# Key-query scores shared by both directions of an mLSTM recurrence, and the causal mask as one rounded matrix pass

## The chip, the cores and the metric

The kernel runs on one core of a Trainium2 chip. A core has TensorE (matrix products into the accumulator memory PSUM), VectorE, ScalarE, GpSimd, SyncE and DMA queues; each engine works through its own instructions in order, and semaphores make one wait for another. The metric is the device time of one launch in microseconds (us), lower is better. Before the change it was 3623.95 us, the median of 3 runs (3618.31 to 3626.76).

## The reference

Two networks run one after the other. The first has two layers; in each, the 512 tokens and 256 context tokens are projected, and three mixers work on the result: a Fourier mix, an mLSTM recurrence in both directions, and an attention. An output projection and an MLP follow. The second network (two layers of another kind) is not touched. The recurrence is what the change is about:

```python
def step(carry, inp):
    C, n, m = carry
    qb, kb, vb, ib, fb = inp
    b = jnp.cumsum(fb, axis=-1)
    dmat = jnp.where(tri, b[..., :, None] - b[..., None, :] + ib[..., None, :], -jnp.inf)
    inter = b + m[..., None]
    m_t = jnp.maximum(inter, dmat.max(axis=-1))
    w_intra = jnp.exp(dmat - m_t[..., None])
    w_inter = jnp.exp(inter - m_t)
    s = jnp.einsum("bhtd,bhsd->bhts", qb, kb) * w_intra
    num = jnp.einsum("bhts,bhsv->bhtv", s, vb) + w_inter[..., None] * jnp.einsum("bhtd,bhdv->bhtv", qb, C)
    den = s.sum(axis=-1) + w_inter * jnp.einsum("bhtd,bhd->bht", qb, n)
    h = num / jnp.maximum(jnp.abs(den), jnp.exp(-m_t))[..., None]
    ...
    C_new = decay[..., None, None] * C + jnp.einsum("bhs,bhsd,bhsv->bhdv", wk, kb, vb)
```

`fwd` and `bwd` take the same `q`, `k` and `v`; only the gates, the mask (`tri`, lower or upper) and the order of the chunks differ. There are 4 heads of 96 features.

## The kernel before

All work is float32. Most large products are done as three rounded passes (`hi` and `lo` parts of a number, in a type that TensorE takes in one pass, fp32r); the small ones of the recurrence are true float32 products, and the trace shows each such matmul as two TensorE records.

`build` calls, for each of the two layers, `fourier`, `latent_attention`, `mlstm_inputs`, `mlstm` (here), `out_projection` and the MLP. Each is a block of instructions with a part for every engine; no block begins before the one before it is through on all engines, so nothing of `out_projection` runs beside `mlstm`. No weights are loaded inside `mlstm`; the only DMA is a small table (`select`).

`mlstm` works on tiles of 128 tokens. There are `TT` = 6 of them (`LT` = 4 latent tiles, 0 to 3, and 2 of context, 4 and 5). `ORDER` walks them as 4, 5, 0, 1, 2, 3 forward and 5, 4, 3, 2, 1, 0 backward. `steps_all` is the list of twelve steps, forward and backward in turn: u = 2 i + d is position i of direction d. `outs` are the steps that give an output: all 12 in the first layer, and in the second, where the context is no longer needed, the 8 from i = 2 on. `upds` are the 10 steps that update a state (i below 5). An output step does:

- `weigh(u)` on TensorE, three groups of matmuls: the mask (L1715, one matmul of the 128 x 128 identity with the mask spread over 4 heads, 128 x 512), the selection of the row exponents (L1718, 4 matmuls with 36 rows), and the key-query scores (L1724, 4 matmuls with 96 rows). Mask and selection add up in one PSUM bank, the scores have another; both pairs of banks alternate;
- ScalarE takes the exponential of the first bank (L1786, 4 instructions);
- VectorE multiplies scores and weights (L1817, `scored_step`);
- `sums(u)` on TensorE: products with the values (L1736, 128 rows), and, for i above 0, with the state (L1742, 96 rows);
- VectorE combines and normalises (`combine`, L1828 to L1844) and signals `written`; TensorE's next `sums` waits for that;
- `grow(u)` on TensorE (L1753, 128 rows), with keys weighted by GpSimd (L1691), and VectorE's `pass_on` (L1856, L1858) update the state;
- where a tile has been visited from both sides, VectorE adds up its squares (`moments`, L1865, L1866).

The order is written out by hand. TensorE runs, for each step, `weigh` of the next output step, then `sums` and `grow` of this one. VectorE runs `scored_step` of the next output step, then `combine`, `pass_on` and, where due, `moments` of this one. After the last step the normed tiles are gated, turned on TensorE (L1771) and copied (L1796).

Below, an output step is a first visit if its tile has not been seen by the other direction, and a second visit otherwise. In the first layer the twelve are F F S S F F F F S S S S, in the second F F F F S S S S.

Of the kernel before, what the change touches and what calls it, by code (L numbers as in the profile page):

```python
# [20 lines left out]
F32R = mybir.dt.float32r  # L21
ALU = mybir.AluOpType
ACT = mybir.ActivationFunctionType
AX = mybir.AxisListType

P = 128
D = 1024
KT = D // P
# [3 lines left out]
ALL = LAT + CTX  # L32
LT, CT = LAT // P, CTX // P
TT = LT + CT

F_GROUP = D // 16
M_HEADS, M_DIM = 4, 3 * D // 32
# [44 lines left out]
C_IDENT, C_LOWER, C_UPPER, C_DFT, C_END = 0, P, 2 * P, 3 * P, 5 * P  # L82
# [1540 lines left out]
    k_turned.close(TT)  # L1623


def mlstm(core, arena, scratch, m, mix, ctx_out):

# [8 lines left out]
    a = Alloc(scratch, 4192 + ROWS * TT)  # L1638
    weight, score = a(2, M_HEADS * P), a(2, M_HEADS * P)
    keyed = a(2, hid)  # L1640
    part, both = a(1, M_HEADS * (M_DIM + 1)), a(2, M_HEADS * (M_DIM + 1))
    state = a(2, M_HEADS * (M_DIM + 1))
    den, ms = a(2, M_HEADS), a(1, TT * M_HEADS)[:, 0, :]
    sq = a(1, hid)[:, 0, :]
    ai = m.rows_i[0:ROWS, :]
    tile = lambda ap, t: ap[:, t * P:(t + 1) * P]
    scale = float(M_DIM) ** -0.5
# [4 lines left out]
    upds = [u for u, (d, i, t) in enumerate(steps_all) if i < TT - 1]  # L1652

    done_at = lambda t: max(u for u in outs if steps_all[u][2] == t)
    tiles_done = sorted(range(nt), key=done_at)
    n_out = lambda u: sum(v < u for v in outs)
    n_upd = lambda u: sum(v < u for v in upds)
# [4 lines left out]
    turned = core.counter("gate_rows_turned")  # L1662
    select_in = core.counter("select_in")
    weights_p = core.counter("weight_exponents")
    scores_p = core.counter("mlstm_scores")
    w_exp = core.counter("weights_ready")
    scored = core.counter("weighted_scores")
    summed = core.counter("mlstm_sums")
# [7 lines left out]
    with nc.Block(no_gpsimd_drain=True) as block:  # L1676
# [19 lines left out]
        @block.tensor  # L1696
        def _(pe):
            for q, rows in enumerate((ai, m.w_state, m.floor, m.w_key)):
                for t in range(TT):
                    n = q * TT + t  # L1700
                    last = nc.tensor.transpose(core.ps[:, 4 + n // 12, n % 12 * ROWS:(n % 12 + 1) * ROWS],
                                               tile(rows, t), core.ident(ROWS))
            last = nc.tensor.matmul(core.ps[:, 6, 0:ROWS * TT], core.ones[0:ROWS, :],
                                    m.decay_rows.rearrange("p r t -> p (r t)"), start=True, stop=True)
            last.then_inc(turned.sem, 1)
            pe.wait_ge(select_in.sem, select_in.at(16))

            def weigh(u):

                d, i, t = steps_all[u]  # L1710
                n = n_out(u)
                if n >= 2:
                    pe.wait_ge(w_exp.sem, w_exp.at(n - 1))
                mask = core.const[:, C_UPPER:C_UPPER + P] if d == 0 else core.const[:, C_LOWER:C_LOWER + P]
                nc.tensor.matmul(core.ps[:, n % 2, :], core.ident(P), mask[:, None, :].to_broadcast([P, M_HEADS, P]),  # L1715
                                 start=True, stop=False)
                for h in range(M_HEADS):
                    last = nc.tensor.matmul(core.ps[:, n % 2, h * P:(h + 1) * P], select[0:ROWS, d * M_HEADS + h, :],  # L1718
                                            tile(m.top, t), start=False, stop=h == M_HEADS - 1)
                last.then_inc(weights_p.sem, 1)  # L1720
                if n >= 2:
                    pe.wait_ge(scored.sem, scored.at(n - 1))
                for h in range(M_HEADS):
                    last = nc.tensor.matmul(core.ps[:, 2 + n % 2, h * P:(h + 1) * P], tile(m.k[0:M_DIM, h, :], t),  # L1724
                                            tile(m.q[0:M_DIM, h, :], t), start=True, stop=True)
                last.then_inc(scores_p.sem, 1)

            def sums(u):
                d, i, t = steps_all[u]
                n = n_out(u)  # L1730
                pe.wait_ge(scored.sem, scored.at(n + 1))
                if n >= 1:
                    pe.wait_ge(written.sem, written.at(n))
                for h in range(M_HEADS):
                    c = slice(h * (M_DIM + 1), (h + 1) * (M_DIM + 1))
                    last = nc.tensor.matmul(core.ps[:, 4 + n % 2, c], score[:, n % 2, h * P:(h + 1) * P],  # L1736
                                            m.v[:, t, h, :], start=True, stop=True)
                if i:
                    pe.wait_ge(passed.sem, passed.at(n_upd(2 * (i - 1) + d) + 1))
                    for h in range(M_HEADS):  # L1740
                        c = slice(h * (M_DIM + 1), (h + 1) * (M_DIM + 1))
                        last = nc.tensor.matmul(core.ps[:, 6, c], tile(m.q[0:M_DIM, h, :], t), state[0:M_DIM, d, c],  # L1742
                                                start=True, stop=True)
                last.then_inc(summed.sem, 1)

            def grow(u):
                d, i, t = steps_all[u]
                n = n_upd(u)
                pe.wait_ge(keys.sem, keys.at(n + 1))
                if n >= 1:  # L1750
                    pe.wait_ge(passed.sem, passed.at(n))
                for h in range(M_HEADS):
                    last = nc.tensor.matmul(core.ps[0:M_DIM, 7, h * (M_DIM + 1):(h + 1) * (M_DIM + 1)],  # L1753
                                            keyed[:, n % 2, h * M_DIM:(h + 1) * M_DIM], m.v[:, t, h, :],
                                            start=True, stop=True)
                last.then_inc(grown.sem, 1)

            pe.wait_ge(token_rows.sem, token_rows.at(3))
            weigh(outs[0])
            for u in range(len(steps_all)):  # L1760
                n = n_out(u)
                if u in outs and n + 1 < len(outs):
                    weigh(outs[n + 1])
                if u in outs:
                    sums(u)
                if u in upds:
                    grow(u)
            for n, t in enumerate(tiles_done):
                pe.wait_ge(normed.sem, normed.at(n + 1))
                for j in range(3):  # L1770
                    last = nc.tensor.transpose(core.ps[:, t, j * P:(j + 1) * P], out[:, t, j * P:(j + 1) * P],  # L1771
                                               core.ident(P))
                last.then_inc(y_turned.sem, 1)

        @block.scalar
        def _(act):
            for u in outs:
                d, i, t = steps_all[u]
                n = n_out(u)
                if n == 0:  # L1780
                    act.wait_ge(token_rows.sem, token_rows.at(2))
                act.wait_ge(weights_p.sem, weights_p.at(n + 1))
                if n >= 2:
                    act.wait_ge(scored.sem, scored.at(n - 1))
                for h in range(M_HEADS):
                    last = nc.scalar.activation(weight[:, n % 2, h * P:(h + 1) * P],  # L1786
                                                core.ps[:, n % 2, h * P:(h + 1) * P], ACT.Exp,
                                                bias=per_token[:, t, ROW0[d] + h:ROW0[d] + h + 1])
                last.then_inc(w_exp.sem, 1)
            for n, t in enumerate(tiles_done):  # L1790
                act.wait_ge(mean_sq.sem, mean_sq.at(n + 1))
                g = ms[:, t * M_HEADS:(t + 1) * M_HEADS]
                nc.scalar.activation(g, g, ACT.Sqrt, bias=core.eps[:, 0:1], scale=1.0 / M_DIM).then_inc(root.sem, 1)
# [6 lines left out]
        def _(dve):  # L1800
# [8 lines left out]
            heads = lambda ap: ap.rearrange("p (h d) -> p h d", h=M_HEADS)  # L1809

            def scored_step(u):
                n = n_out(u)
                dve.wait_ge(w_exp.sem, w_exp.at(n + 1))
                dve.wait_ge(scores_p.sem, scores_p.at(n + 1))
                if n >= 2:
                    dve.wait_ge(summed.sem, summed.at(n - 1))
                v.scalar_tensor_tensor(score[:, n % 2, :], core.ps[:, 2 + n % 2, :], scale, weight[:, n % 2, :],  # L1817
                                       ALU.mult, ALU.mult).then_inc(scored.sem, 1)

            def combine(u):  # L1820
# [68 lines left out]
            chain.close(step.n)  # L1889
    no, nu = len(outs), len(upds)  # L1890
    for s, k in ((mean_sq, nt), (root, nt), (normed, nt), (gated, 1), (turned, 1), (select_in, 16), (weights_p, no),
                 (scores_p, no), (w_exp, no), (scored, no), (summed, no), (keys, nu), (grown, nu), (passed, nu),
                 (written, no), (token_rows, 3), (y_turned, nt)):
        s.close(k)

# [582 lines left out]
def build(nc, dram, stop=None):  # L2478
    with ExitStack() as ctx:
# [14 lines left out]
        for l in range(DEPTH):  # L2494
# [3 lines left out]
            with core.space("arena", [P, ARENA]) as arena:  # L2498
                mix = arena[:, 0:KT * ALL].rearrange("p (k n) -> p k n", k=KT)
                with parts(ALL) as (h, acts):  # L2500
# [4 lines left out]
                    m = Mlstm(arena, mix)  # L2505
                    acc = arena[:, 2 * ALL:2 * ALL + 2 * (CONV_IN - 4)].rearrange("p (a n) -> p a n", a=2)
                    mlstm_inputs(core, arena, acts, l, m, acc)
                with core.space("scratch", [P, 2 * KT * ALL]) as scratch:
                    mlstm(core, arena, scratch, m, mix, not last)
                with parts(ALL) as (h, acts):  # L2510
                    tmp = arena[:, KT * ALL:(KT + 2) * ALL].rearrange("p (a n) -> p a n", a=2)
                    mod = None
# [230 lines left out]
```

## Time and profile before

| | |
|---|---|
| median of 3 runs | 3623.95 us (3618.31 to 3626.76) |
| profiled execution | 3622.27 us |
| span in its trace | 3620.5 us |
| TensorE busy | 3278.1 us, 91% |
| VectorE / ScalarE / GpSimd busy | 1779.8 / 1108.8 / 275.5 us |
| `mlstm`, first layer | about 405.4 to 499.6 us of the span |
| `mlstm`, second layer | about 1480.1 to 1555.3 us |
| mean granted clock of TensorE | 0.957 of full speed |

How to read it: PE is TensorE's matmul record, DVE VectorE, ACT ScalarE, POOL GpSimd. "L1715" is a line of the kernel. A row of a timeline merges neighbouring instructions of one line; its duration runs to the end of the last one, and ends of matmuls overlap the start of the next, so the time that a group takes in the queue is read from its start to the next start. PEclk in a row of windows is the clock granted to TensorE: 1.00 is 2.4 GHz, 0.50 is 1.2 GHz.

### The profile page before, as it was taken

What the parts mean: (1) busy time and instruction counts of PE and PEld (TensorE: products, weight loads), DVE (VectorE), ACT (ScalarE), POOL (GpSimd) and SP (SyncE); (2) the same over time, 40 slices, a digit from 0 to 9 for tenths busy, and PEclk for the clock granted to TensorE, in tenths of its full rate; (3) what the DMA queues carried; (4) which work ended last, traced back from release to release, by engine and by line L of the source; (5) the groups of instructions that cost most, each with busy time, mean ns of one, the idle gap of its engine ahead of it and who ended that gap; (6) DMA issues with size and microseconds to landing.
All of it is one profiled execution on the core that took longest, in us unless ns stands there. A gap on an engine that the chain in (4) does not pass through costs nothing. (4 is left out here: it accounts for less than half of the span.)

```text
span 3620.5 us, 52487 instructions
## 1 busy us (share of the span) xinstructions
PE 3278.1 (91%) x20898; PEld 2866.3 (79%) x20898; DVE 1779.8 (49%) x2649; ACT 1108.8 (31%) x1647; POOL 275.5 (8%) x234
## 2 busy tenths in 40 slices
PE   1999986999997899879999699889999899889997
PEld 1668775888886578758887697789999897789997
DVE  8547578554545647553333434544343434444343
ACT  2243223232232243223333333233222432233222
POOL 2000101001001000111111200010101100000101
PEclk9999888999998999889999899999999999999998
DMA  6101023322323101012222111122222211122322
GB/s 243 59 9 59 25 83 116 117 104 104 116 104 145 58 20 62 11 59 93 93 93 81 66 48 41 38 74 88 98 91 89 77 42 44 51 76 82 104 82 87
DMA packets 79090, 283.40 MB, mean 78 GB/s; under 512 B 10584, under 2 KB 10712, under 8 KB 77280
## 3 DMA queue, kind: packets, MB, share of 16 engines
q1 hardware_dynamic: 74912, 264.48, 20.7%
q0 software_dynamic: 3168, 11.31, 0.9%
q10 hardware_dynamic: 864, 5.57, 0.4%
q8 instruction: 102, 1.67, 0.2%
q14 instruction: 44, 0.36, 0.0%
HBM read 279.20 MB, written 2.10 MB: 78 GB/s over the span
## 5 line engine op out<-in xcount | busy, mean ns | idle before, releaser
L311 PE MATMUL ps<-h_hi,hi_ring 128*128 128x264 f32 (+2 forms) x4208 | 1344.9, 320 | 99.8 <-DVE h_lo L601 42.7
L311 PE MATMUL ps<-h_lo,hi_ring 128*128 128x264 f32 (+2 forms) x4208 | 1312.8, 312 | 0.0
L311 PE MATMUL ps<-h_hi,lo_ring 128*128 128x264 f32 (+2 forms) x4208 | 1310.5, 311 | 0.0
L240 DVE TENSOR_TENSOR lo_ring<-ring,hi_ring 128x1024 fp32r<-128x1024 f32 (+1 forms) x414 | 491.7, 1188 | 1036.2 <-ACT hi_ring L230 1035.3
L311 PEld LDWEIGHTS ps<-h_hi,hi_ring 128*128 128x128 f32 (+1 forms) x4208 | 796.6, 189 | 186.6 <-issue 108.7
L311 PEld LDWEIGHTS ps<-h_lo,hi_ring 128*128 128x128 f32 (+1 forms) x4208 | 798.2, 190 | 50.5 <-issue 3.4
L311 PEld LDWEIGHTS ps<-h_hi,lo_ring 128*128 128x128 f32 (+1 forms) x4208 | 794.5, 189 | 47.0
L230 ACT ACTIVATE hi_ring<-ring 128x1024 fp32r<-128x1024 f32 (+1 forms) x414 | 424.5, 1025 | 1265.1 <-PE ps L311 1244.2
L311 PE MATMUL ps<-hid_hi,hi_ring 128*128 128x512 f32 (+1 forms) x1472 | 473.4, 322 | 2.6 <-DVE hid_lo L839 1.7
L311 PE MATMUL ps<-hid_lo,hi_ring 128*128 128x512 f32 (+1 forms) x1472 | 474.2, 322 | 0.0
L311 PE MATMUL ps<-hid_hi,lo_ring 128*128 128x512 f32 (+1 forms) x1472 | 474.2, 322 | 0.0
L311 PEld LDWEIGHTS ps<-hid_hi,hi_ring 128*128 128x128 f32 x1472 | 276.2, 188 | 27.3 <-DVE hid_lo L839 1.9
L311 PEld LDWEIGHTS ps<-hid_lo,hi_ring 128*128 128x128 f32 x1472 | 276.7, 188 | 23.4
L311 PEld LDWEIGHTS ps<-hid_hi,lo_ring 128*128 128x128 f32 x1472 | 276.7, 188 | 22.2
L549 POOL TENSOR_TENSOR sumsq<-sumsq,sq 128x528 f32<-128x528 f32 (+2 forms) x116 | 175.5, 1513 | 1087.3 <-ACT sq L534 1085.3
L421 DVE SCALAR_TENSOR_TENSOR silu_rows<-mod_ring,silu_rows 128x1024 f32<-128x1024 f32 x128 | 161.9, 1309 | 187.3 <-DMA mod_ring<-w_mod_dram 187.2
L534 ACT ACTIVATE sq<-x 128x768 f32<-128x768 f32 (+3 forms) x128 | 90.1, 705 | 334.0 <-DVE x L667 209.0
L300 PE MATMUL ps<-sumsq,ones 128*128 128x264 f32 (+2 forms) x34 | 23.5, 836 | 139.9 <-PEq L476 63.3
L300 PEld LDWEIGHTS ps<-sumsq,ones 128*128 128x128 f32 x34 | 9.7, 322 | 147.5 <-issue 81.8
L421 DVE SCALAR_TENSOR_TENSOR arena<-arena 128x1024 f32<-128x1024 f32 x64 | 85.9, 1404 | 0.0
L2309 DVE TENSOR_REDUCE arena<-ps 128x1 f32<-128x400 f32 (+4 forms) x56 | 31.4, 561 | 106.3 <-PE ps L2073 95.8
L667 DVE SCALAR_TENSOR_TENSOR x<-ps,mod,x 128x512 f32<-128x512 f32 x120 | 75.2, 654 | 0.1
(277 smaller groups left out, 2998.1 us busy)
## 6 DMA issues: line engine op xcount, KB each, us to landing
ring<-weights_dram SPq DMA_DIRECT2D x350, 512.0 KB, 3.2
mod_ring<-w_mod_dram SPq DMA_DIRECT2D x64, 512.0 KB, 4.1
ring<-weights_dram SPq DMA_DIRECT2D x64, 384.0 KB, 2.9
arena<-w_mod_dram SPq DMA_DIRECT2D x32, 512.0 KB, 3.4
x<-x_dram SPq DMA_DIRECT2D x1, 3072.0 KB, 16.2
arena<-c_rows_dram ACTq DMA_DIRECT2D x3, 1024.0 KB, 7.2
arena<-ret_decay_dram POOLq DMA_DIRECT2D x2, 1056.0 KB, 7.1
silu_rows<-c_rows_dram ACTq DMA_DIRECT2D x2, 1024.0 KB, 5.3
```

The source lines that it names most:

```text
L230: self.nc.scalar.activation(self.hi_ring[:, g % SPLIT, 0:w], self.ring[:, g % RING, 0:w], ACT.Copy).then_inc(self.hi, 1)
L240: self.nc.vector.tensor_tensor(self.lo_ring[:, g % SPLIT, 0:w], self.ring[:, g % RING, 0:w], self.hi_ring[:, g % SPLIT, 0:w], ALU.subtract ...
L300: ins = nc.tensor.matmul(out[row:row + m, c:c + n], w, a[:, t0:t0 + n], start=first and k == 0, stop=last and k == len(weights) - 1)
L311: ins = nc.tensor.matmul(out[0:m, c:c + n], w, a[:, t0:t0 + n], start=first and k == 0 and p == 0, stop=last and k == kts - 1 and p == 2)
L421: core.nc.vector.scalar_tensor_tensor(self.scratch[:, c, :], self.ring[:, g % MOD_RING, :], 1.0, self.rows[:, c, :], ALU.mult, ALU.mult, a ...
L534: core.nc.scalar.activation(tmp[:, i % 2, 0:n], core.x[:, m, 0:n], ACT.Square).then_inc(self.squared.sem, 1)
L549: core.nc.gpsimd.tensor_tensor(dst, dst, src, ALU.add).then_inc(core.added.sem, 1)
L667: ins = v.scalar_tensor_tensor(dst, s, gate(c), dst, ALU.mult, ALU.add)
L2309: v.tensor_reduce(columns(top, u), src, AX.X, ALU.max, negate=True).then_inc(peak.sem, 1)
```

## The change

Two edits in `mlstm`, and the room for them:

- the scores of a tile are computed at its first visit alone, copied by ScalarE from PSUM into `qk_scores` (new, one 128 x 512 slot per tile), and read there by VectorE at both visits;
- ScalarE copies identity and both masks into `masks`, of the type fp32r, once at the block's start, and the mask matmul takes these: one rounded pass in place of the float32 product;
- `part` and `sq` move into memory that the convolution has left free, and `scratch` gives up 3 x 128 columns for `masks`.

```diff
-    part, both = a(1, M_HEADS * (M_DIM + 1)), a(2, M_HEADS * (M_DIM + 1))
-    state = a(2, M_HEADS * (M_DIM + 1))
+    both, state = a(2, M_HEADS * (M_DIM + 1)), a(2, M_HEADS * (M_DIM + 1))
     den, ms = a(2, M_HEADS), a(1, TT * M_HEADS)[:, 0, :]
-    sq = a(1, hid)[:, 0, :]
+    qk_scores = a(TT, M_HEADS * P)
+    b = Alloc(m.conv[0].rearrange("p a n -> p (a n)"))
+    part, sq = b(1, M_HEADS * (M_DIM + 1)), b(1, hid)[:, 0, :]
...
+    firsts = [u for u in outs if all(steps_all[w][2] != steps_all[u][2] for w in outs if w < u)]
+    first_of = {steps_all[u][2]: n for n, u in enumerate(firsts)}
...
                 if n >= 2:
                     pe.wait_ge(w_exp.sem, w_exp.at(n - 1))
-                mask = core.const[:, C_UPPER:C_UPPER + P] if d == 0 else core.const[:, C_LOWER:C_LOWER + P]
-                nc.tensor.matmul(core.ps[:, n % 2, :], core.ident(P), mask[:, None, :].to_broadcast([P, M_HEADS, P]),
+                mask = masks[:, 2 if d == 0 else 1, :]
+                nc.tensor.matmul(core.ps[:, n % 2, :], masks[:, 0, :], mask[:, None, :].to_broadcast([P, M_HEADS, P]),
                                  start=True, stop=False)
...
-                if n >= 2:
-                    pe.wait_ge(scored.sem, scored.at(n - 1))
+                if u not in firsts:
+                    return
+                s = firsts.index(u)
+                if s >= 2:
+                    pe.wait_ge(scores_in.sem, scores_in.at(s - 1))
                 for h in range(M_HEADS):
-                    last = nc.tensor.matmul(core.ps[:, 2 + n % 2, h * P:(h + 1) * P], tile(m.k[0:M_DIM, h, :], t),
+                    last = nc.tensor.matmul(core.ps[:, 2 + s % 2, h * P:(h + 1) * P], tile(m.k[0:M_DIM, h, :], t),
                                             tile(m.q[0:M_DIM, h, :], t), start=True, stop=True)
...
             pe.wait_ge(token_rows.sem, token_rows.at(3))
+            pe.wait_ge(masks_in.sem, masks_in.at(1))
             weigh(outs[0])
...
         def _(act):
+            nc.scalar.activation(masks[:], core.const[:, 0:3 * P].rearrange("p (r n) -> p r n", r=3),
+                                 ACT.Copy).then_inc(masks_in.sem, 1)
...
                 last.then_inc(w_exp.sem, 1)
+                if u in firsts:
+                    s = firsts.index(u)
+                    act.wait_ge(scores_p.sem, scores_p.at(s + 1))
+                    nc.scalar.activation(qk_scores[:, s, :], core.ps[:, 2 + s % 2, :], ACT.Copy
+                                         ).then_inc(scores_in.sem, 1)
...
-                n = n_out(u)
+                n, s = n_out(u), first_of[steps_all[u][2]]
                 dve.wait_ge(w_exp.sem, w_exp.at(n + 1))
-                dve.wait_ge(scores_p.sem, scores_p.at(n + 1))
+                dve.wait_ge(scores_in.sem, scores_in.at(s + 1))
                 if n >= 2:
                     dve.wait_ge(summed.sem, summed.at(n - 1))
-                v.scalar_tensor_tensor(score[:, n % 2, :], core.ps[:, 2 + n % 2, :], scale, weight[:, n % 2, :],
+                v.scalar_tensor_tensor(score[:, n % 2, :], qk_scores[:, s, :], scale, weight[:, n % 2, :],
                                        ALU.mult, ALU.mult).then_inc(scored.sem, 1)
...
-                with core.space("scratch", [P, 2 * KT * ALL]) as scratch:
-                    mlstm(core, arena, scratch, m, mix, not last)
+                with core.space("scratch", [P, 2 * KT * ALL - 3 * P]) as scratch, \
+                        core.space("masks", [P, 3, P], F32R) as masks:
+                    mlstm(core, arena, scratch, masks, m, mix, not last)
```

TensorE's queue at the start of the first layer's recurrence, before (`ps` is PSUM, `const` holds identity and masks, `scratch` and `arena` are memory; L1715 mask, L1718 selection, L1724 scores, L1736 and L1742 the two parts of `sums`, L1753 `grow`):

```order
L1715 MATMUL ps<-const 128x512
L1718 MATMUL ps<-arena,scratch 128x128 x4
L1724 MATMUL ps<-arena 128x128 x4
L1736 MATMUL ps<-arena,scratch 128x97 x4
L1753 MATMUL ps<-arena,scratch 96x97 x4
L1715 MATMUL ps<-const 128x512
L1718 MATMUL ps<-arena,scratch 128x128 x4
L1724 MATMUL ps<-arena 128x128 x4
L1736 MATMUL ps<-arena,scratch 128x97 x4
L1742 MATMUL ps<-scratch,arena 128x97 x4
L1753 MATMUL ps<-arena,scratch 96x97 x4
```

The same place after the change (the third and fourth `weigh`; the lines have moved: L1719 is the mask, L1722 the selection, L1743 and L1749 `sums`, L1760 `grow`):

```order
L1719 MATMUL ps<-masks 128x512
L1722 MATMUL ps<-arena,scratch 128x128 x4
L1743 MATMUL ps<-arena,scratch 128x97 x4
L1760 MATMUL ps<-arena,scratch 96x97 x4
L1719 MATMUL ps<-masks 128x512
L1722 MATMUL ps<-arena,scratch 128x128 x4
L1743 MATMUL ps<-arena,scratch 128x97 x4
L1749 MATMUL ps<-scratch,arena 128x97 x4
L1760 MATMUL ps<-arena,scratch 96x97 x4
```

Both are second visits, so the four score matmuls between selection and sums are gone, and the mask reads `masks`. ScalarE's queue in the first layer (L1786 and L1796 the exponentials before and after, L1785 the rounding of the masks, L1803 the copy of the scores):

```order
-L1775 UNCONDITIONAL_BRANCH
-L1786 ACTIVATE scratch<-ps,scratch 128x128 x48
-L1793 ACT_TABLE_LOAD
...
+L1783 UNCONDITIONAL_BRANCH
+L1785 ACTIVATE masks<-const 128x384
+L1796 ACTIVATE scratch<-ps,scratch 128x128 x4
+L1803 ACTIVATE scratch<-ps 128x512
+L1796 ACTIVATE scratch<-ps,scratch 128x128 x4
+L1803 ACTIVATE scratch<-ps 128x512
+L1796 ACTIVATE scratch<-ps,scratch 128x128 x12
+L1803 ACTIVATE scratch<-ps 128x512
```

A copy now stands behind the four exponentials of each first visit: 6 copies in the first layer and 4 in the second.

## Rows read from the trace of the kernel before

**Rows 1.** the page: each engine's busy us, share of the span and instructions.

```profile
PE 3278.1 (91%) x20898; PEld 2866.3 (79%) x20898; DVE 1779.8 (49%) x2649; ACT 1108.8 (31%) x1647; POOL 275.5 (8%) x234
```

**Rows 2.** windows: us, then busy us of PE, PEld, DVE, ACT, POOL; PEclk; DMA.

```profile
410.20:426.40 16.20, 16.20 (x54) 11.43 (x54) 3.48 (x8) 2.29 (x8) 4.00 (x4) 0.50 0.00 1
427.00:477.00 50.00, 50.00 (x383) 41.97 (x382) 39.39 (x88) 10.88 (x39) 5.78 (x7) 1.00 0.00 1
1499.20:1501.60 2.40, 2.40 (x6) 0.90 (x5) 1.11 (x2) 0.00 (x0) 1.20 (x1) 0.50 0.00 0
1502.00:1536.00 34.00, 34.00 (x262) 28.61 (x261) 25.20 (x57) 7.24 (x26) 3.30 (x4) 1.00 0.00 1
1335.00:1340.00 5.00, 3.36 (x27) 2.72 (x26) 0.71 (x3) 1.50 (x3) 0.00 (x0) 1.00 0.00 0
```

**Rows 3.** timeline of PE, a step at 2.4 GHz: start, us, engine, line, operation.

```profile
457.73 1.05 PE L1715 MATMUL ps<-const 128*128 128x512 f32 x2
458.71 1.16 PE L1718 MATMUL ps<-arena,scratch 36*128 36x128 f32 x8
459.79 1.16 PE L1724 MATMUL ps<-arena 96*128 96x128 f32 x8
460.79 1.03 PE L1736 MATMUL ps<-arena,scratch 128*128 128x97 f32 x8
461.66 1.06 PE L1742 MATMUL ps<-scratch,arena 96*128 96x97 f32 x8
462.55 0.85 PE L1753 MATMUL ps<-arena,scratch 128*96 128x97 f32 x8
463.23 1.05 PE L1715 MATMUL ps<-const 128*128 128x512 f32 x2
```

**Rows 4.** timeline of DVE: two steps without a wait, and a later wait.

```profile
440.44 0.68 DVE L1817 SCALAR_TENSOR_TENSOR scratch<-ps,scratch 128x512 f32<-128x512 f32 x1
441.04 0.55 DVE L1828 TENSOR_TENSOR scratch<-ps,scratch 128x388 f32<-128x388 f32 x1
...
446.61 0.55 DVE L1828 TENSOR_TENSOR scratch<-ps,scratch 128x388 f32<-128x388 f32 x1
...
457.25 0.56 DVE L1828 TENSOR_TENSOR scratch<-ps,scratch 128x388 f32<-128x388 f32 x1 [0.98 <-PE ps L1742]
```

**Rows 5.** timeline of PE, the first layer's start at 1.2 GHz.

```profile
412.17 2.07 PE L1718 MATMUL ps<-arena,scratch 36*128 36x128 f32 x8
414.17 2.07 PE L1724 MATMUL ps<-arena 96*128 96x128 f32 x8
416.04 1.91 PE L1715 MATMUL ps<-const 128*128 128x512 f32 x2
417.88 2.07 PE L1718 MATMUL ps<-arena,scratch 36*128 36x128 f32 x8
...
421.75 1.86 PE L1736 MATMUL ps<-arena,scratch 128*128 128x97 f32 x8
423.41 1.50 PE L1753 MATMUL ps<-arena,scratch 128*96 128x97 f32 x8
424.70 1.96 PE L1715 MATMUL ps<-const 128*128 128x512 f32 x2
```

**Rows 6.** timeline of PE after the first layer's main steps, again at 1.2 GHz.

```profile
482.49 1.99 PE L1736 MATMUL ps<-arena,scratch 128*128 128x97 f32 x8 [3.27 <-DVE scratch L1844]
484.28 1.91 PE L1742 MATMUL ps<-scratch,arena 96*128 96x97 f32 x8
```

**Rows 7.** timeline of PE in the projection that follows, at 1.2 GHz.

```profile
1558.54 0.63 PE L311 MATMUL ps<-h_hi,hi_ring 128*128 128x512 f32 x1
1558.96 0.63 PE L311 MATMUL ps<-h_lo,hi_ring 128*128 128x512 f32 x1
```

**Rows 8.** lines by form: a copy out of PSUM on ACT, count, busy us, mean ns.

```profile
L819 ACT ACTIVATE tmp<-ps 128x512 f32<-128x512 f32 x32 | 18.6, 581 | 0.0
```

**Rows 9.** lines by form, DVE: a product with both operands in memory.

```profile
L650 DVE SCALAR_TENSOR_TENSOR x<-x,param,sumsq 128x512 f32<-128x512 f32 x8 | 5.4, 748 | 0.0
```

More of the change, by code:

```diff
@@ L1623, in mlstm_inputs, with mlstm @@
     k_turned.close(TT)
-def mlstm(core, arena, scratch, m, mix, ctx_out):
+def mlstm(core, arena, scratch, masks, m, mix, ctx_out):
     nc, dram = core.nc, core.dram
@@ L1664, in mlstm @@
     weights_p = core.counter("weight_exponents")
-    scores_p = core.counter("mlstm_scores")
+    scores_p, scores_in = core.counter("mlstm_scores"), core.counter("mlstm_scores_copied")
+    masks_in = core.counter("mlstm_masks_rounded")
     w_exp = core.counter("weights_ready")
@@ L1891, in mlstm @@
     for s, k in ((mean_sq, nt), (root, nt), (normed, nt), (gated, 1), (turned, 1), (select_in, 16), (weights_p, no),
-                 (scores_p, no), (w_exp, no), (scored, no), (summed, no), (keys, nu), (grown, nu), (passed, nu),
+                 (scores_p, len(firsts)), (scores_in, len(firsts)), (masks_in, 1), (w_exp, no), (scored, no), (summed, no), (keys, nu), (grown, nu), (passed, nu),
                  (written, no), (token_rows, 3), (y_turned, nt)):
```

## The prediction

> **What bounds the kernel now.** I read four views, in this order. The page first: TensorE is busy 3278.1 us, 91% of the span, VectorE 1779.8 [rows 1], so TensorE bounds the program as a whole; the change touches two stretches of it, some 78 and 62 us long. Then the windows. In the main steps of the first layer (427 to 477 us) PE is busy all 50.00 us at a granted clock of 1.00, VectorE 39.39; in the second layer (1502 to 1536) PE is busy 34.00 of 34.00, VectorE 25.20. But the 16.20 us before the first of these are also all busy, and their clock is 0.50; so are the 2.40 us of the second layer's first prefetched mask [rows 2]. The third view, PE's timeline, gives one step at 2.4 GHz: mask 0.98 us (457.73 to 458.71), selection 1.08, scores 1.00, sums with the values 0.87, sums with the state 0.89, `grow` 0.68; together 5.50 us from mask to mask [rows 3]. The fourth is VectorE's timeline. Where a step has all its instructions (combining, state, squares) VectorE too needs 446.61 - 441.04 = 5.57 us; later it waits 0.98 us for L1742 at each step [rows 4]. So TensorE sets the pace, and VectorE stands right behind it where a second visit is combined.
>
> **The change, part by part, at the clock as it was.** The mask loses one of its two records and half the passes of the other. A rounded 128 x 512 matmul follows its like after 1558.96 - 1558.54 = 0.42 us at 1.2 GHz [rows 7], hence 0.21 at 2.4. Of the old mask's time (0.98 at 2.4, 1.84 at 1.2, from 416.04 to 417.88 [rows 3, 5]) four such pieces are 0.84 and 1.68; I keep the rest, about 0.14, for the change of group. The new mask takes 0.35 and 0.56 us and saves 0.63 and 1.28. Bounds: 0.77 saved at 2.4 GHz if that rest goes too, nothing if a rounded matmul ahead of a float32 one is held up. Twenty masks.
>
> The scores go in 10 of 20 output steps: 1.00 us each at 2.4 GHz, 1.87 at 1.2 (414.17 to 416.04) [rows 3, 5]. That leaves TensorE 4.87 us for a step with a first visit in `weigh` and 3.87 with a second.
>
> Added on ScalarE: ten copies, 0.58 us each by a copy of the same shape out of PSUM [rows 8]. ScalarE was busy 10.88 of 50 us [rows 2]. The copy starts once the four exponentials (1.14 us, 2.29 for two sets [rows 2]) and the scores are through; VectorE's product, which now waits for it, comes 1.14 + 0.58 = 1.7 us behind the selection, while TensorE needs 1.00 + 0.87 + 0.89 = 2.8 us for scores and sums before `combine` can start. So the copy is hidden, except at each stretch's start, where nothing else is under way: 0.6 us twice. Were it exposed at each first visit it would cost 10 x 0.58 = 5.8 us. Behind VectorE's product in its queue stands `combine` of the step before, and TensorE waits for that.
> The rounding of the masks on ScalarE falls into its idle time before the first exponential; at most 0.5 us if ScalarE came late to the block. VectorE's product reads memory instead of PSUM: a product of that size with both operands in memory takes 0.75 us [rows 9], against 441.04 - 440.44 = 0.60 from the old product's start to the next instruction's [rows 4]; that one has a column operand too, so I take no change, and at the most 20 x 0.15 = 3 us more. The wait for a free scores bank is on an earlier copy and is over long before. Nothing changes for POOL, SP or the DMAs.
>
> What becomes late next is VectorE. A second visit costs it 5.57 us and stays at that; after a first visit the chain `written` -> sums (0.87 + 0.89) -> combine (about 2.4) with its signals is some 4.4 us. At 2.4 GHz, TensorE's second-visit `weigh` therefore buys about 1.1 us (5.50 to 4.4) where it falls beside a first-visit combine, and nothing where it falls beside a second-visit one. If the clock rises where it did: first layer 3 masks at 1.2 GHz, 3.8 us, four first-visit steps of 0.63, 2.5 us, two of 1.1, 2.2 us: 8.5, less the 0.6; second layer 1.3 + 2 x 0.63 + 3 x 1.1 = 5.9, less the 0.6. Together 13 us less.
>
> **The clock, on which the result turns.** What was TensorE doing before the clock rose? In the first layer it ran selections (36 rows), scores (96 rows), two masks, sums, without a gap for 13 us, and stayed at 1.2 GHz; it rose right behind `grow` and a whole four-pass mask, 1.29 and some 1.9 us of 128-row streaming (from 423.41) [rows 5]. In the second layer too it is a mask at 0.50 (from 1499.20), and 1.00 from 1502 on [rows 2]. My reading, an inference from these two places: both rises stand behind dense 128-row streaming, and none behind the narrow products, however busy PE was with them. The change takes three quarters of that one dense piece away, and of a second visit's scores all. What is left at 1.2 GHz: mask 0.56, selection 2.00, scores 1.87, sums 1.66, sums with the state about 1.8 (1.91 busy), `grow` 1.29 [rows 5, 6]. In the first layer's first two steps there is no product with the state, so scores, sums, `grow` and mask stand back to back; there the clock may still rise. In the second layer each step has its 96-row state product and 36-row selection between the dense groups, and I expect it to stay low.
>
> The Trainium skill ("TensorE: Matmul & The Clock Gate", Part 1: The HAM clock gate) has the default state throttled and says that activity releases it, by how busy the engine has been. By that rule 16.20 us of full busy time would not have stayed at 0.50, and the changed kernel, still busy, would warm up as before: 13 us less. The trace disagrees for these narrow matmuls, and I go by it, but leave that outcome its chance.
>
> What a low clock costs. Second layer, from its second mask to `sums` of the seventh output: three first-visit weighs of 4.43 us, four second-visit ones of 2.56, six times sums, state and `grow` at 4.75: 13.3 + 10.2 + 28.5 = 52.0 us. Before, that was seven weighs and six groups, from 1499.2: 2.3 + 34.0 in the two windows and what lies around them, about 37.3. So +14.7, less the 1.3 that the first mask saves, plus 1.6 for the last sums at half speed: **+15**. First layer, if it stays low to the end: six first-visit weighs 26.6, six others 15.4, ten sums 16.6, eight state products 14.4, ten `grow` 12.9: 85.9 against 16.2 + 50.0 + about 1: +18.7, and 1.6 at the end: **+20**. TensorE is then the bound in every step, 9.2 or 7.3 us against VectorE's 5.57.
>
> **The rivals and their chances.** The profiled execution (3622.27 us) is 1.7 us under the median, so I add the differences to 3623.95.
>
> - Forecast: first layer rises as before (-8), second stays at 1.2 GHz (+15): +7, 3631 us. For it: the pair of plain steps that only the first layer has. Its own range is 3625 to 3638 (a rise late in the second layer, or one step later in the first). Chance 0.36.
> - Both stay low: +35, 3659 us. The decision falls in the first two steps of layer one; where the dense run is cut by the selection at the wrong moment, nothing later makes up for it. Chance 0.22.
> - Mixed: the clock rises in the middle of a stretch, or drops and comes back. Between, +10 to +25, about 3641. Chance 0.13.
> - Faster, the other side: the clock rises in both layers where it did. -13, 3611 us. For it: rows 2, where PE at 3.36 busy of 5.00 holds 1.00 (1335 to 1340), show that once up it is not lost to short gaps, and at a clock of 1.00 all my terms are gains; against it, the 16 us above. It decides from the point where the second layer's first full step is left at 1.00. Chance 0.26.
> - The change does not do what it says at the clock given: the rounded mask is held up, or the copies are exposed (5.8) and eat the gain: within 3 us of before. Chance 0.03.
>
> A measurement of this kernel tells 0.2%, 7.2 us, from no change. Faster by more: most of the fourth case, 0.25. Slower by more: the second and third cases and half of the first, 0.53. The rest, 0.22, is same. The range is 3608 to 3662: it takes in the gain of the fourth case and both low stretches, and leaves at most 2 in 10 out.
>
> **What the profile after would show.** The mask as one record per step, 0.2 to 0.3 us to the selection at 2.4 GHz; ten copies of about 0.58 us on ScalarE; VectorE's product waiting for one only at the start. The deciding rows are the windows: a clock of 0.50 over most of the second layer's stretch, with PE busy throughout and steps of 7 to 9 us, makes my forecast right; a clock of 1.00 from the second full step, PE busy 70 to 90% and a wait for VectorE of about 1.5 us before L1743 in second visits makes it wrong, and the time then lies near 3611.

## The result, and the profile after

The changed kernel takes 3634.9 us (median of 15 runs, 3624.32 to 3650.17), the kernel before 3620.2 us (15 runs, 3612.78 to 3626.76): ratio 1.0042, 95% interval 1.0029 to 1.0055. It is slower by some 15 us, 10 to 20 by the interval. The spread of single times is 26 us, against 14 before. Over the 15 runs the time goes with TensorE's mean granted clock: 0.950 and 0.949 in the two fastest (3624.32 and 3624.53 us), 0.940 and 0.942 in the two slowest (3649.91 and 3650.17). The profiled execution took 3629.29 us, with a span of 3627.5 us; it is the third fastest of the 15.

The windows from the first selection of each recurrence to the first turned tile give the two stretches. Columns as in [rows 2]: us, busy us of PE, PEld, DVE, ACT and POOL with counts, granted clock, DMA share, GB/s. First the changed kernel:

```profile
409.40:493.20 83.80, 72.68 (x412) 66.17 (x411) 54.59 (x121) 19.84 (x61) 8.95 (x11) 0.66 0.00 1
1486.60:1558.40 71.80, 58.87 (x312) 53.60 (x311) 41.42 (x90) 13.83 (x41) 8.02 (x9) 0.62 0.00 1
```

then the kernel before, cut in the same way:

```profile
412.20:491.80 79.60, 70.77 (x472) 58.90 (x471) 54.19 (x122) 16.46 (x55) 7.86 (x10) 0.84 0.00 1
1486.50:1550.10 63.60, 51.94 (x352) 43.80 (x351) 40.79 (x90) 11.51 (x37) 7.36 (x8) 0.82 0.00 1
```

The reader is to see two things. TensorE has 100 records fewer and is busy for longer (131.6 us against 122.7), because its clock went from 0.84 and 0.82 to 0.66 and 0.62. And VectorE's work is what it was. The first stretch is 4.2 us longer, the second 8.2: 12.4 us, more than the 7 us by which this execution's time exceeds the profiled one of before. The windows begin behind the first mask, so the 1.28 us that it saves in each layer lie outside them; the rest of the gap lies elsewhere in the two executions.

Where the clock changed, read from finer windows of the changed kernel:

```profile
408.70:443.00 34.30, 34.30 (x150) 30.99 (x150) 14.12 (x30) 7.49 (x23) 5.53 (x6) 0.50 0.00 1
443.20:470.00 26.80, 24.35 (x198) 21.88 (x197) 23.48 (x54) 8.29 (x27) 4.13 (x5) 1.00 0.00 1
470.60:480.00 9.40, 9.40 (x44) 8.74 (x44) 7.43 (x16) 2.64 (x7) 0.00 (x0) 0.50 0.00 1
1487.00:1514.80 27.80, 24.94 (x115) 22.75 (x115) 9.16 (x17) 5.21 (x15) 5.14 (x6) 0.50 0.00 1
1515.00:1525.00 10.00, 9.28 (x80) 8.51 (x80) 8.14 (x18) 2.83 (x9) 1.65 (x2) 1.00 0.00 1
1525.30:1542.00 16.70, 16.70 (x77) 15.13 (x76) 11.29 (x25) 2.28 (x8) 0.83 (x1) 0.50 0.01 1
```

Against [rows 2] the first layer stays at 1.2 GHz for 34.30 us in place of 16, all of it busy, and the second for some 28 in place of some 17 (from its first mask, 1484.52, to about 1502). New is the third and the sixth row: in both layers the clock is lost again while second visits run. In the second layer it comes back at 1542, in the fourth of them. TensorE's timeline shows one step at each level and what stood before the loss (start, us, engine, line; L1719 mask, L1722 selection, L1743 and L1749 sums, L1760 `grow`):

```profile
426.29 0.77 PE L1719 MATMUL ps<-masks 128*128 128x512 f32 x1
426.99 2.07 PE L1722 MATMUL ps<-arena,scratch 36*128 36x128 f32 x8
429.00 2.02 PE L1743 MATMUL ps<-arena,scratch 128*128 128x97 f32 x8
430.81 1.91 PE L1749 MATMUL ps<-scratch,arena 96*128 96x97 f32 x8
432.52 1.50 PE L1760 MATMUL ps<-arena,scratch 128*96 128x97 f32 x8
433.72 0.77 PE L1719 MATMUL ps<-masks 128*128 128x512 f32 x1
...
462.69 0.48 PE L1719 MATMUL ps<-masks 128*128 128x512 f32 x1
463.10 1.16 PE L1722 MATMUL ps<-arena,scratch 36*128 36x128 f32 x8
464.98 1.10 PE L1743 MATMUL ps<-arena,scratch 128*128 128x97 f32 x8 [0.73 <-DVE scratch L1856]
465.92 1.06 PE L1749 MATMUL ps<-scratch,arena 96*128 96x97 f32 x8
466.82 0.85 PE L1760 MATMUL ps<-arena,scratch 128*96 128x97 f32 x8
467.44 0.48 PE L1719 MATMUL ps<-masks 128*128 128x512 f32 x1
467.85 1.16 PE L1722 MATMUL ps<-arena,scratch 36*128 36x128 f32 x8
470.12 1.69 PE L1743 MATMUL ps<-arena,scratch 128*128 128x97 f32 x8 [1.11 <-DVE scratch L1859]
```

A step with a second-visit `weigh` takes 433.72 - 426.29 = 7.43 us at 1.2 GHz and 467.44 - 462.69 = 4.75 at 2.4, where before it took 5.50 [rows 3]. The edit does what it says. The mask is one record, but 0.70 us to the selection at 1.2 GHz and 0.41 at 2.4. Just before the loss TensorE waits for VectorE (0.73 and 1.11 us; in the second layer 0.72), behind a selection of 36 rows. Whether the waits or the thin work lost the clock is taken up with e1 and e4.

VectorE's product and ScalarE's new work in the first layer, by line and form:

```profile
L1832 DVE SCALAR_TENSOR_TENSOR scratch<-scratch 128x512 f32<-128x512 f32 x12 | 8.2, 687 | 15.7 <-ACT scratch L1803 10.3 <-ACT scratch L1796 5.4
L1803 ACT ACTIVATE scratch<-ps 128x512 f32<-128x512 f32 x6 | 3.6, 597 | 2.5 <-PE ps L1731 2.5
L1785 ACT ACTIVATE masks<-const 128x384 fp32r<-128x384 f32 x1 | 0.5, 524 | 3.3 <-PEq L1416 3.3
```

VectorE's product (L1832) costs 0.687 us from memory, as it did from PSUM, and waits 15.7 us in all, before 16.1. At 1.2 GHz it waits for ScalarE's copy; TensorE, which sets the pace there, is busy all the while.

### The profile page after: what moved, and what is told of

Same layout as the page of the kernel before. It is cut to its first block and busy times, and to the rows that moved or that the text cites. A ratio compares the mean times of both kernels' runs of the same rounds, so it can differ in the third digit from the quotient of the medians.

```text
span 3627.5 us, 52299 instructions
## 1 busy us (share of the span) xinstructions
PE 3283.6 (91%) x20798; PEld 2883.0 (79%) x20798; DVE 1781.5 (49%) x2649; ACT 1114.9 (31%) x1659; POOL 275.9 (8%) x234
```

## The experiments

The question left by the result: is it the clock, as forecast, or the work and waits of the new instructions? All kernels below were timed beside the kernel before, on one of three chips; ratios are to it, with the 95% interval. "Stretches" are the two windows defined above, added up, in the one profiled execution, whose time is in the column ahead of them; they were 143.2 us before and 155.6 after.

| kernel | median us | before us | ratio | profiled us | stretches us | clock in them |
|---|---|---|---|---|---|---|
| e1 float32 mask, shared scores | 3620.94 | 3626.74 | 0.9984 (0.9974 to 0.9993) | 3624.34 | 139.1 | 0.84, 0.77 |
| e2 rounded mask, scores each visit | 3633.14 | 3626.74 | 1.0021 (1.0007 to 1.0034) | 3629.07 | 150.2 | 0.81, 0.66 |
| e3 mask 4 times, 128 rows | 3622.69 | 3626.74 | 0.9989 (0.9980 to 0.9999) | 3623.99 | 138.2 | 0.88, 0.76 |
| e4 same, 3 of 4 with 32 rows | 3681.37 | 3626.74 | 1.0156 (1.0125 to 1.0186) | 3699.11 | 213.4 | 0.51, 0.50 |
| e5 mask 3 times | 3622.41 | 3625.88 | 0.9991 (0.9969 to 1.0012) | 3625.88 | 142.3 | 0.82, 0.73 |
| e6 warm start and fill | 3623.10 | 3625.88 | 0.9991 (0.9981 to 1.0001) | 3614.16 | 128.3 | 0.93, 0.89 |
| e7 warm start only | 3627.60 | 3625.88 | 0.9999 (0.9981 to 1.0017) | 3629.15 | 149.1 | 0.71, 0.70 |
| e8 changed kernel again | 3634.99 | 3625.88 | 1.0025 (1.0008 to 1.0041) | 3661.22 | 180.8 | 0.50, 0.54 |
| e9 warm start, mask twice | 3620.35 | 3624.46 | 0.9987 (0.9976 to 0.9998) | 3619.49 | 137.0 | 0.90, 0.72 |
| e10 e1 with the warm start | 3613.47 | 3624.46 | 0.9971 (0.9960 to 0.9982) | 3612.86 | 131.1 | 0.91, 0.83 |
| e11 kernel before, warm start | 3616.99 | 3624.46 | 0.9975 (0.9959 to 0.9990) | 3620.63 | 131.4 | 0.92, 0.93 |

A profiled execution is one sample: e8's is the slowest of its 12 runs, e4's the fifth of 6, e6's the fastest of its 12; the others lie within 6 us of their medians.

**e1: the float32 mask back, the scores shared.**

```diff
-                mask = masks[:, 2 if d == 0 else 1, :]
-                nc.tensor.matmul(core.ps[:, n % 2, :], masks[:, 0, :], mask[:, None, :].to_broadcast([P, M_HEADS, P]),
+                mask = core.const[:, C_UPPER:C_UPPER + P] if d == 0 else core.const[:, C_LOWER:C_LOWER + P]
+                nc.tensor.matmul(core.ps[:, n % 2, :], core.ident(P), mask[:, None, :].to_broadcast([P, M_HEADS, P]),
```

> The mask goes back to the float32 product of identity and mask (two records, four passes); the scores stay shared and copied by ScalarE. Clock theory: the dense 128-row stretch behind grow is back, so the clock rises in both layers about where it did before, and the saved scores count at 2.4 GHz: 3 to 8 us faster than before, some 20 us faster than the changed kernel. Rival (the loss comes from the shared scores: ScalarE's copy exposed, VectorE waiting for it): still slower than before, +10 us or more, since that part is untouched. Rival (work alone): slower than the changed kernel by 20 x 0.63 = 13 us.

Measured: 0.9984, about 6 us faster than before. Its two windows:

```profile
412.30:488.30 76.00, 65.15 (x423) 53.50 (x422) 53.58 (x122) 19.82 (x61) 7.45 (x9) 0.84 0.00 1
1492.80:1555.90 63.10, 49.96 (x319) 41.57 (x318) 40.72 (x90) 13.84 (x41) 7.35 (x8) 0.77 0.00 1
```

More passes on the bounding engine, and a faster kernel: both rivals fall. The shared scores and their copies are a small gain when the mask stays dense. On the loss of the clock this kernel says two things. In the first layer the granted clock is 1.00 from 426.4 to 474 us, although in second visits TensorE waits for VectorE for 0.48 and 0.93 us. In the second layer it holds through all second visits but the last, and falls at 1542, right behind the same wait of 0.93 us.

**e2: the rounded mask alone.** The scores are made in every step and read from PSUM.

```diff
-                if u not in firsts:
-                    return
-                s = firsts.index(u)
-                if s >= 2:
-                    pe.wait_ge(scores_in.sem, scores_in.at(s - 1))
+                s = n
+                if n >= 2:
+                    pe.wait_ge(scored.sem, scored.at(n - 1))
...
-                dve.wait_ge(scores_in.sem, scores_in.at(s + 1))
+                dve.wait_ge(scores_p.sem, scores_p.at(n + 1))
```

> The mask is the one rounded pass of the change; the scores are made at every visit and read from PSUM as before, without a copy. Clock theory: the mask alone takes the dense stretch away, so long parts of both layers stay at 1.2 GHz: +8 to +20 us against before, near the changed kernel. Rival (the shared scores cause the loss): faster than before by 20 x 0.63 = 13 us less what is hidden, some 8 to 12 us.

Measured: 1.0021, slower by 2.5 to 12 us; the middle, 7.6 us, lies just under the 8 to 20 expected. The sign decides: the cheaper mask by itself costs time. Its two windows:

```profile
409.50:487.10 77.60, 67.29 (x461) 61.18 (x460) 53.22 (x122) 16.57 (x55) 9.68 (x11) 0.81 0.00 1
1484.80:1557.40 72.60, 60.16 (x345) 55.15 (x344) 41.80 (x90) 11.62 (x37) 8.27 (x10) 0.66 0.00 1
```

The loss is about half of the changed kernel's. In this profile the clock rises late (429 and 1525 us) but then stays at 1.00 until TensorE has only the last sums left; in the changed kernel's it is also lost in second visits. So the thin mask delays the rise, and that the clock is lost again seems to need the missing scores as well; one profile of each kernel is too little to show it.

**e3 and e4: the same extra matmuls, wide and narrow.** In e3:

```diff
+                for _ in range(3):
+                    nc.tensor.matmul(core.ps[:, n % 2, :], masks[0:P, 0, :],
+                                     mask[0:P, None, :].to_broadcast([P, M_HEADS, P]), start=True, stop=True)
                 nc.tensor.matmul(core.ps[:, n % 2, :], masks[:, 0, :], mask[:, None, :].to_broadcast([P, M_HEADS, P]),
                                  start=True, stop=False)
```

In e4 `0:32` stands for `0:P`, and 32 for the first P of the shape.

> The changed kernel, with three extra rounded mask matmuls (128 rows, 128 x 512, overwritten at once) ahead of the real one in each step: 60 matmuls of pure extra work on the bounding engine, 0.21 us each at 2.4 GHz, 13 us. Clock theory: the clock rises in both layers as before, and the time is 2 to 8 us under before, some 20 us under the changed kernel, although work was added. Rival (work alone, or the float32 product was special): 13 to 25 us slower than the changed kernel.

> As the kernel with the mask four times, but the three extra matmuls have 32 rows instead of 128; columns, count, and TensorE's busy time are the same. Clock theory as I read the rows of before (wide rows raise it, busy time alone does not): the clock stays low about as in the changed kernel, and the extra 60 x 0.43 us at 1.2 GHz come on top: +25 to +40 us against before. Rival (busy time or streamed columns raise the clock, whatever their rows): as with 128 rows, 2 to 8 us under before.

Measured: 0.9989 and 1.0156. With sixty useless matmuls the changed kernel is faster than the kernel before, by 4 us (0.4 to 7); the same sixty with a quarter of the rows make it some 57 us slower than before, more than expected. The windows of e3:

```profile
411.80:484.50 72.70, 62.15 (x445) 54.69 (x444) 53.95 (x122) 19.74 (x61) 7.23 (x9) 0.88 0.00 1
1485.90:1551.40 65.50, 52.17 (x334) 46.26 (x333) 40.70 (x90) 13.88 (x41) 7.36 (x8) 0.76 0.00 1
```

and of e4, with the same 445 and 334 records on PE and a larger busy share:

```profile
411.50:530.90 119.40, 110.71 (x445) 93.12 (x444) 57.71 (x122) 20.05 (x61) 7.23 (x9) 0.51 0.00 1
1533.20:1627.20 94.00, 82.44 (x334) 70.01 (x333) 42.72 (x90) 13.90 (x41) 7.35 (x8) 0.50 0.00 1
```

TensorE is busy 93% of e4's first stretch and holds 0.51; in e3 it is 85% and 0.88. It is not busy time that raised the clock here. This pair is the strongest evidence of the study.

Three shorter windows of e4 bear on the loss of the clock:

```profile
409.30:424.80 15.50, 15.50 (x56) 12.28 (x56) 2.45 (x6) 3.48 (x10) 2.47 (x3) 0.50 0.01 1
424.90:427.90 3.00, 3.00 (x18) 2.22 (x19) 0.95 (x2) 0.58 (x3) 1.11 (x1) 1.00 0.00 0
428.40:460.00 31.60, 31.60 (x128) 26.84 (x128) 16.57 (x33) 4.69 (x15) 2.48 (x3) 0.50 0.00 1
```

The clock rose for 3 us and fell again while TensorE did not stop for a moment (15.50 of 15.50, 3.00 of 3.00, 31.60 of 31.60 us busy). So it can be lost to the kind of work alone, without a wait. Whether the waits of 0.7 to 1.1 us have a share in the loss in the changed kernel stays open: e1 went through like waits in one layer and lost the clock behind one in the other, and no run takes them away.

**e5, e7: less filling, or only a start.** e5 is e3 with `range(2)`. e7 adds to the changed kernel, while TensorE would wait for VectorE's row copies:

```diff
-            pe.wait_ge(token_rows.sem, token_rows.at(3))
             pe.wait_ge(masks_in.sem, masks_in.at(1))
+            for _ in range(8):
+                nc.tensor.matmul(core.ps[:, 0, :], masks[:, 0, :],
+                                 masks[:, 1, None, :].to_broadcast([P, M_HEADS, P]), start=True, stop=True)
+            pe.wait_ge(token_rows.sem, token_rows.at(3))
```

> As the kernel with the mask four times, with two extra 128-row matmuls in place of three. Clock theory: still enough dense streaming behind grow for the clock to rise, with 20 x 0.21 us less added work: 4 to 9 us under before. Rival (only the amount of the old mask does it): the clock stays low in part, 0 to +12 us.

> The changed kernel with 8 extra rounded 128-row matmuls at the start of each recurrence and nothing else, to tell the rise from the holding of the clock. Clock theory: where the rise is the whole matter, 5 to 8 us under before; where the thinner second-visit steps can also lose the clock once it is up, some of it is given back: between -6 and +6 us, with single executions well above. Rival: +11 us against before plus the added 3 us a layer.

Measured: e5 0.9991, its interval takes in 1, so it can't be told from before or from e3. e7 0.9999: by the medians the start alone gives back 7 of the 9 us that e8, the changed kernel on the same chip, lies above before; the intervals of the two overlap. Its single times lie between 3613 and 3644 us. In its profile the clock was up and lost again in both layers (0.71, 0.70 on average): the rise is one matter, holding it another. Nor is the start sure: in the first layer the eight matmuls ran from 407.11 to 410.68 us, and the clock was still 0.50 until 422.4, with TensorE busy throughout; in the second the selection behind them took 1.08 us, so it was up. The slot is not wholly idle either: the changed kernel stands still there for 1.55 us, the eight take 3.57.

**e6, e9: start and filling together.** e6 has 12 matmuls at the start, and four ahead of the mask in the first three output steps and in every second visit; e9 has 8 at the start and one ahead of each mask.

> The changed kernel with 12 extra rounded 128-row matmuls while TensorE waits for VectorE's row copies at the start of each recurrence, and four extra ones ahead of the mask in the first three output steps and in each second visit, where TensorE has slack at 2.4 GHz; none in the other first visits. Clock theory: 2.4 GHz from the first steps on and never lost; 6 to 10 us under before. Rival (work alone): 24 x 0.43 at the start and some 60 x 0.21 us more than the changed kernel, +25 us or more against before.

> The changed kernel with 8 extra rounded 128-row matmuls at the start of each recurrence and the rounded mask issued twice in every step. Clock theory: the first lift the clock, the second (0.21 us a step) keep it through the thin second-visit steps: the whole gain of about 13 us that the change has at 2.4 GHz, less some 3 us of added work: 7 to 13 us under before. Rival (the warm start alone, measured at no difference from before, is all there is to get): within 4 us of before.

Measured: 0.9991 and 0.9987, by the middle values 3 and 5 us, half of what was expected. e6's interval takes in 1, so it can't be told from before; its rival (+25 us) is out. e9 is 1 to 9 us under before, and that does not separate what was expected (7 to 13) from its rival (within 4). The profiled execution of e6 had the shortest stretches of all, 128.3 us at 0.93 and 0.89, 15 us under before; its median is only 3 us under. Two things account for that. The extra matmuls at the start lie ahead of the windows: from the start of the last small product before the recurrence's steps to the first selection e6 takes 7.54 and 6.69 us in the two layers, the kernel before 4.64 in each, 5 us more in all. And this execution is the fastest of e6's twelve, 8.9 us under their median, with the highest mean granted clock of them (0.958, the others 0.953 to 0.956).

**e8: the changed kernel again.**

> The changed kernel unaltered, beside the three above on the same chip: +8 to +18 us against before, with a wider spread of single times than before's, since the clock rises at another place from execution to execution.

Measured: 1.0025 (1.0008 to 1.0041), 9 us by either measure, 3625.95 to 3661.22 us in 12 runs. The wider spread that was expected is not clear here: the kernel before spreads over 35 us as well on this chip (35 runs), through three runs of 3641 to 3648 us whose mean granted clock is 0.948 to 0.950, against 0.957 to 0.959 in its three fastest. So it, too, has executions at a lower clock. e8's profiled execution, the slowest of its 12, is one in which the first layer never rose:

```profile
410.90:512.90 102.00, 93.37 (x412) 85.36 (x411) 56.97 (x122) 20.00 (x61) 9.00 (x11) 0.50 0.00 1
1511.60:1590.40 78.80, 65.45 (x313) 59.82 (x313) 42.45 (x91) 13.98 (x41) 7.98 (x9) 0.54 0.00 1
```

102.0 and 78.8 us against 79.6 and 63.6: +22.4 and +15.2. The rival "both stay low" was priced at +20 and +15, +35 together; this execution lies 35 us over before's median.

**e10, e11: the best version, and what of it is the change's.** e10 is e1 with the eight matmuls at the start (`masks` kept for them). e11 is the kernel before with two float32 mask matmuls at that place and nothing else.

> Shared scores, float32 mask, and the same 8 matmuls at the start. Clock theory: the clock rises one to three steps earlier than with the float32 mask alone: 6 to 10 us under before. Rival (the warm-up costs what it gives): as the float32 mask alone, 5 to 6 us under.

> The kernel before, with two extra float32 mask matmuls (as many passes as the eight) at the start of each recurrence and nothing of the change. Clock theory: 2.4 GHz from the first steps on: 4 to 9 us under before, so that a part of what the combined versions gain is not the change's. Rival: within 2 us of before, or slower by the added 3 us a layer.

Measured: 0.9971 and 0.9975. e10 is 11 us under before by the medians, the fastest of all, at 0.91 and 0.83 in its profile:

```profile
414.70:484.50 69.80, 58.85 (x423) 48.43 (x422) 54.00 (x122) 19.66 (x61) 6.61 (x8) 0.91 0.00 1
1482.50:1543.80 61.30, 46.84 (x320) 38.72 (x319) 41.42 (x90) 13.74 (x41) 7.35 (x8) 0.83 0.00 1
```

But e11 gains 7 us by the medians with no saved work, and the intervals of the two overlap. The start alone (e11, 7 us) and the shared scores alone (e1, 6 us) do not add up in e10 (11 us); that the shared scores give anything on top of the start is not shown, though e10's median lies 3.5 us under e11's.

## Why the prediction was right

- **The bound and the terms.** TensorE's steps shrank much as worked out. A step with a first-visit `weigh` takes 4.87 us at 2.4 GHz (forecast 4.87) and 9.14 at 1.2 (9.2); one with a second-visit `weigh` 7.43 at 1.2 (7.3). At 2.4 it takes 4.75 where the chain through VectorE was put at 4.4, so it saves 0.75 us, not 1.1. The mask's saving was a little over-sized: the change of group costs 0.20 us at 2.4 GHz and 0.28 at 1.2, not 0.14, so it saves 0.57 and 1.14 us, not 0.63 and 1.28; over twenty masks 1 to 3 us. (The "0.2 to 0.3 us" that the prediction gives at its end for the new mask does not agree with the 0.35 of its own sum; 0.41 was measured.)
- **The copies** take 0.597 us, not 0.58, and VectorE waited for one for 0.16 us at the one place where it did in the stretch at 2.4 GHz; hidden, as forecast. Even the 0.6 us at each stretch's start does not show on TensorE, which goes from scores to sums without a gap (415.83 + 1.87 = 417.70). The product from memory costs what it did.
- **The clock.** The step on which the sign hung, that the clock would not rise where it had, is shown: e1 brings it back with the mask alone, e2 loses it with the mask alone, e3 and e4 tell wide from narrow. The rule of the Trainium skill that was weighed against it (activity, as busyness, releases the throttle; "TensorE: Matmul & The Clock Gate", Part 1: The HAM clock gate) fits e3 and not e4, where 15.50 of 15.50 us busy stood at 0.50 and the clock fell at 31.60 of 31.60 busy; the measurement decides.
- **Where it happened was wrong, and the number owes something to luck.** The forecast's case was: the first layer rises as before and gains 8, the second stays low and loses 15. Neither half came about in the profile. The first layer lost 4.2 us, because its clock stayed at 1.2 GHz for 18 us longer; the plain steps with scores, sums, `grow` and mask in a row, for which I expected the rise, ran at 1.2. The second lost 8.2, and its clock did rise, at 1515 and again at 1542. That is the "mixed" case (+10 to +25, chance 0.13), and +15 lies in it, twice the forecast's +7. Over executions the clock's place varies, so the median is a mix of cases: of those with a slower kernel, +7, +17 (the mixed case's 3641) and +35 had 0.36, 0.13 and 0.22. The "faster" case (-13, 0.26) did not come near: none of the 15 runs is under 3624.32, 4 us above before's median.
- **"Once up it is not lost to short gaps" was wrong.** I took it from a window in which PE held 1.00 with 3.36 of 5.00 us busy [rows 2]. In second visits of the changed kernel the clock went at 470 and 1525 us, and ran at 0.50 for the rest of the first layer's steps and for 17 us of the second's. Whether the short gaps did it stays open (e1). What the sentence left out is shown by e4: the work itself, with TensorE busy all the time, can lose the clock.

## What to carry to other kernels

A TensorE whose clock depends on what it streams can lose more by a cheaper instruction than the instruction saves: before removing dense 128-row work from a stretch of thin products, read the granted clock ahead of and inside that stretch. Where a stage starts at 1.2 GHz with thin products, a few dense matmuls at its start, where the engine would wait anyway, are worth a trial of their own, and they should be tried on the unchanged kernel first (here 0.9975; in e7's first layer they did not raise the clock). Time such a kernel in many runs: one profile shows one of several places of the rise.

## What the runs showed of the hardware that was not expected

- In e4 the granted clock rose to 1.00 for 3 us and fell to 0.50 again with TensorE busy without a gap.
- With 32-row matmuls in each step the clock stayed low nearly all the time (0.51 and 0.50). Every one of e4's six runs (3662.55 to 3705.02 us) is above every run of the changed kernel (3661.22 at most). An estimate for a clock that never rises is the prediction's +35 and 20 x 1.58 us for the extra group (431.20 - 429.62 in e4's timeline), +67 us; +55 was measured by the medians and +72 in the profiled execution. Whether the thin work itself pushes the clock down or only takes longer was not separated.
- Eight dense matmuls at the start (3.57 us) did not raise the clock in the first layer of e7's profile, while in e9 and e11 as many passes did: there the clock came up in the first selection behind them, which took 1.49 and 1.26 us, between 2.00 at 1.2 GHz and 1.08 at 2.4.
- A rounded mask matmul ahead of float32 ones costs 0.70 us at 1.2 GHz and 0.41 at 2.4 to the next group, where its like in a row of rounded ones takes 0.42 at 1.2 [rows 7].
